# Block 2's feed-forwards: the second-matrix units moved apart, and other PSUM banks for them

## The reference, cut to what matters

```python
gate, up = jnp.split(x @ w_ffn_in[i], 2, axis=-1)      # 1024 -> 2 x 2816
ffn = (jax.nn.silu(gate) * up) @ w_ffn_out[i]          # 2816 -> 1024
x = layer_norm(ALPHA * x + ffn + ple, ln2_g[i], ln2_b[i])
```

## Time and profile before

| | us |
|---|---|
| median of three runs | 2522.41 |
| the profiled execution's own time | 2535.36 |
| its span, first to last instruction | 2533.6 |
| PE busy in the span | 2440.2 (96%) |
| DVE busy | 1771.5 (70%) |
| ACT busy | 1094.8 (43%) |
| POOL busy | 1067.2 (42%) |

### The profile page before, as it was taken

The page is one execution under the profiler, slowest core; times in us unless marked ns, Lnnn a source line. Parts: engine busy times, 40 slices in busy tenths (PEclk is TensorE's granted clock), DMA queues, the critical chain, the costliest instruction groups (busy, mean ns, idle before and its releaser), DMA issues.

```text
span 2533.6 us, 35157 instructions
## 1 busy us (share of the span) xinstructions
PE 2440.2 (96%) x13615; PEld 2044.6 (81%) x13615; DVE 1771.5 (70%) x2671; ACT 1094.8 (43%) x1803; POOL 1067.2 (42%) x600
## 2 busy tenths in 40 slices
PE   7999999999999999999999999999999999999997
PEld 5776788978776788998777779999877777999985
DVE  5677777864477687774587478887468747888856
ACT  4335532423425543443443554444444355444442
POOL 0332453424234244444245347544514534754441
PEclk9999999999999999999999999999999999999999
DMA  8613345543321433332232123332323111333321
GB/s 284 200 51 117 117 150 182 189 145 94 109 84 64 142 119 125 101 100 84 85 84 75 51 67 100 125 101 92 100 81 83 59 51 67 117 101 108 102 91 50
DMA packets 239645, 268.87 MB, mean 106 GB/s; under 512 B 19976, under 2 KB 204024, under 8 KB 239224
## 3 DMA queue, kind: packets, MB, share of 16 engines
q1 hardware_dynamic: 239480, 266.63, 32.6%
HBM read 264.51 MB, written 2.10 MB: 105 GB/s over the span
## 4 chain that ended last, share of the span: by engine, by line
PE 71%; DVE 12%; issue 5%; ACT 4%; POOL 4%; DMA 3%; SPq 0%; ACTq 0%; DVEq 0%; POOLq 0%
PE bank L2796 21%; PE bank L2798 21%; PE bank L2797 21%; DVE r L1905 2%; DVE m_cv L2246 2%; DVE k_lo L2054 1%; DMA raw<-in_ffn_w 1%; DMA raw<-in_w_ffn_in 1%; POOL w_lo L1650 1%; POOL k_lo L1661 1%; PE bank L3430 1%; DVE u_sum L2071 1%; ACT k_hi L1104 1%; DMA b_raw<-in_ada_w 1%; ACT w_hi L1050 1%
## 5 line engine op out<-in xcount | busy, mean ns | idle before, releaser
L1661 POOL TENSOR_TENSOR k_lo<-raw,k_hi 128x512 fp32r<-128x512 f32 x297 | 430.4, 1461 | 551.6 <-ACT k_hi L1104 550.5
L1650 POOL TENSOR_TENSOR w_lo<-raw,w_hi 128x2048 fp32r<-128x2048 f32 x53 | 248.7, 4692 | 536.6 <-ACT w_hi L1050 454.6
L1104 ACT ACTIVATE k_hi<-raw 128x512 fp32r<-128x512 f32 x444 | 270.9, 626 | 319.3 <-PE bank L2798 245.9
L2796 PE MATMUL bank<-h_hi,k_lo 128*128 128x256 f32 (+1 forms) x1156 | 371.4, 321 | 3.8 <-DVE k_lo L2054 2.5
L2797 PE MATMUL bank<-h_lo,k_hi 128*128 128x256 f32 (+1 forms) x1156 | 370.2, 320 | 0.0
L2798 PE MATMUL bank<-h_hi,k_hi 128*128 128x256 f32 (+1 forms) x1156 | 370.0, 320 | 0.0
L2796 PE MATMUL bank<-h_hi,w_lo 128*128 128x512 f32 x800 | 325.3, 407 | 8.8 <-DVE h_lo L2014 4.1
L2798 PE MATMUL bank<-h_hi,w_hi 128*128 128x512 f32 x800 | 314.1, 393 | 0.0
L2797 PE MATMUL bank<-h_lo,w_hi 128*128 128x512 f32 x800 | 314.1, 393 | 0.0
L2796 PE MATMUL bank<-f_hi,k_lo 128*128 128x512 f32 x704 | 278.1, 395 | 8.3 <-DVE u_row L2115 2.6
L2796 PE MATMUL bank<-u_t_hi,k_lo 128*128 128x256 f32 x1008 | 282.9, 281 | 1.5 <-POOL k_lo L1661 1.5
(11 more groups left out here) (401 smaller groups left out, 4956.8 us busy)
## 6 DMA issues: line engine op xcount, KB each, us to landing
raw<-in_ffn_w SPq DMA_DIRECT2D x56, 1024.0 KB, 5.4
raw<-in_w_ffn_in SPq DMA_DIRECT2D x44, 1024.0 KB, 5.1
raw<-in_w_in SPq DMA_DIRECT2D x34, 1024.0 KB
b_raw<-in_ada_w SPq DMA_DIRECT2D x32, 1024.0 KB, 5.4
f_raw<-in_w_ffn_out SPq DMA_DIRECT2D x24, 512.0 KB, 3.4
z_a<-in_ada_w SPq DMA_DIRECT2D x4, 2048.0 KB, 14.0
g_raw<-in_ada_w SPq DMA_DIRECT2D x8, 1024.0 KB, 5.2
raw<-in_w_out SPq DMA_DIRECT2D x8, 1024.0 KB
```

Of the source, the lines that this page charges most:

```text
L1104: act.activation(hi, src, ACT.Copy).then_inc(s.f_hi.up, 1)
L1650: pool.tensor_tensor(b.w_lo[p][:, 0:n], b.raw[p][:, 0:n], b.w_hi[p][:, 0:n].bitcast(F32), ALU.subtract)\
L1661: pool.tensor_tensor(lo, src, hi.bitcast(F32), ALU.subtract).then_inc(s.f_lo.up, 1)
L2796: pe.matmul(out, wlo, xhi, start=start, stop=False)
```

## The change

In block 2's plan (`spread` and not `early`) the first of a pair's two downs (j even) moves from behind the gate's unit to between the up side's unit and the gate's; the second (j odd) stays behind the gate's. The pairs concerned are 2 to 9. The order of a pair was "up side, gate, down, down" and becomes "up side, down, gate, down". Outside the tail a down with an even j now uses the banks 4 and 5, one with an odd j 3 and 7, and the plain units of the pairs 9 and 10 use 2 and 6. Plain 0, the Strassen units, the tail and the whole of block 1 keep order and banks. The buffers, the ring, `on_vector` and `summed` are unchanged code, but work on the new list.

```diff
         for i in range(PAIRS):
-            self.units += [("upper" if i in uppers else "plain", i, 0),
-                           ("whole" if early and i == 0 else "seven", i, 0)]
-            self.units += downs[:upto.get(i, 0)]
+            self.units.append(("upper" if i in uppers else "plain", i, 0))
+            inside = 1 if spread and not early and i in upto else 0
+            self.units += downs[:inside]
+            self.units.append(("whole" if early and i == 0 else "seven", i, 0))
+            self.units += downs[inside:upto.get(i, 0)]
             del downs[:upto.get(i, 0)]
...
-        if kind == "plain" and self.spread and not self.early and i == 0:
-            return 3, 7
+        if self.spread and not self.early and u < self.tail:
+            if kind == "plain":
+                return (2, 6) if i else (3, 7)
+            if kind == "down":
+                return (3, 7) if j % 2 else (4, 5)
         return first, first + 1
```

## The result

The changed kernel takes 2535.02 us, median of 7 runs (2530.01 to 2539.01); on the same chip the kernel before takes 2524.02 us, also of 7 (2521.05 to 2531.65). The ratio is 1.0037, with a 95% interval of 1.0020 to 1.0053: 5 to 13 us lost. That is within the 0.5% of "no change", but above the range of 2517 to 2531, and the 2524.1 forecast is 11 us too low.

What follows compares the result with a forecast made beforehand. The prediction took PE, busy 96% of the span, as the bound. Its terms, -1.95 + 0.5 + 3.2 = +1.7 us, put on the median of the runs, gave 2524.1 us, range 2517 to 2531, forecast as no change.

Steps and rivals of the forecast that it cites:

- seven 2's wait: PE's wait in seven 2 for a low part from POOL goes: 0.97 us per layer gained, 1.95 in all.
- transitions: Both downs of a pair now stand behind a Strassen unit: 0.03 us x 8 pairs x 2 layers, 0.5 us lost.
- plain 10's wait: Plain 10 waits for pair 9's products, delayed by seven 10's late load: 1.6 us per layer (0.3 to 2.6), 3.2 both.
- pairs 2 to 8: Steady order: PE's work unchanged, bank choice priced at nothing, DVE's slack hides the rest; nothing taken.
- clock behind a wait: Behind plain 10's wait: no clock term was forecast; nothing was taken beyond the wait itself.
- come just after the down's adds: In each half of a pair DVE's one set of sums follows the down's adds; 12.2 us of work before 15.4.
- Waits of PE for DVE's `x` adds (L2762) in every pair: Sign in the steady pairs that would prove the forecast wrong, as would any difference above 12 us.
- Nothing is given back: PE is full behind it: After plain 10's wait: the 3.2 us for both layers are not recovered, because PE is full.
- The rival in which the moved down waits in its middle: Pair 1's late low halves make the moved down wait about 1 us in both layers: +3.7, 2526.1 us; chance 0.17.
- 2 us were all there was to gain: From plain 0 to the tail PE is nearly full, so any order of units wins at most some 2 us.
- The prediction's estimate from the rule, 2.4 us a sum: By the shared-port lock a DVE sum could wait for a full POOL piece: 2.4 us each, 9.7 for four.
- a wait in every pair: Rival: DVE held by POOL in every unit, losing over 5.5 us per pair; +14, 2536 us at 6.5; chance 0.05.

Runs made afterwards that it cites:

- e7: The kernel before, order and banks untouched, with seven 2's four sums placed one piece earlier in DVE's order: 2528.14 us, ratio 0.9983.
- e3: The changed kernel with seven 8's sums one piece later, plain 10 on banks 3 and 7, the down before it on 0 and 4: 2523.14 us, ratio 0.9985.
- e1: The changed kernel with seven 8's four sums placed one piece later, behind the adds of the down before upper 8: 2533.84 us, ratio 1.0029.
- e6: The changed kernel's new order of downs with the banks of the kernel before: 2549.30 us, ratio 1.0076 to the kernel before.
- e5: e1 with 11 matmuls of the identity, into a bank nobody reads, in place of plain 10's wait: 2536.07 us, ratio 1.0020 to the kernel before.

## Why the prediction was wrong

By its own steps, per layer, with the total of both at the end:

| step | forecast | measured | both |
|---|---|---|---|
| seven 2's wait | -0.97 | -0.96, -0.99 | -1.95 |
| transitions | +0.25 | +0.13, +0.22 (the rest of the stretch) | +0.35 |
| plain 10's wait | +1.6 (0.3 to 2.6) | +2.47, +2.50 | +4.97 |
| pairs 2 to 8 | 0 | +1.62, +1.62 | +3.24 |
| clock behind a wait | 0 | +1.72, 0 | +1.72 |

**The step that failed** is "The pairs 2 to 8, in the steady order", and in it the sentence that in each half of a pair the sums "come just after the down's adds". I took the order of one pair for that of all. `summed` counts pieces, and where a pass has one pair the same count lands on the other side of the adds. Four sums of 0.68 us could have been borne there: M5 is due 4.27 us after the down's end (4.24 in the prediction), and the sums alone would have been done by 1740.86 + 2.7 = 1743.6. With POOL they took 6.9 us (1740.86 to 1747.73). The prediction had both numbers, the 1.77 us of a sum beside POOL and an upper's M5 on bank 3, and set them down as covered because it never walked the one pair where the piece count changes. It also named the sign, "Waits of PE for DVE's `x` adds (L2762) in every pair": it came in one pair only.

**Plain 10's wait** was found with the right mechanism, load and queue, and mis-sized: 2.5 for 1.6 us. The load landed at S + 6.5 (forecast 6.7); what was missing is one sum beside POOL, +1.1, which the bounds held and the value taken did not. (By the prediction's own prices two such sums would make 1.6 + 2.2 = 3.8 us; its bound of 2.6 is the case of one.) The reason given for the value, a chain "measured as a whole", was no reason: in the chain of before POOL was idle while the four sums ran (the first starts at 1794.78, the last is below), as POOL's next piece shows.

```profile
1796.71 0.68 DVE L2074 TENSOR_TENSOR u_sum<-raw,u_sum 128x512 f32<-128x512 f32 x1
...
1799.26 1.42 POOL L1661 TENSOR_TENSOR k_lo<-raw,k_hi 128x512 fp32r<-128x512 f32 x1 [6.84 <-ACT k_hi L1104]
```

**"Nothing is given back: PE is full behind it"** failed in the first layer, by 1.7 us: a unit that was full took longer, at the lower clock. The prediction had put that at nothing without a reason; a wait can cost more than itself.

The forecast is 10.9 us too low. Of these 6.6 are the terms above (+8.3 for +1.7), and 1.6 are the base: more runs moved the median of the kernel before from 2522.41 to 2524.02. The last 2.7 are within the interval of the ratio, and no run shows a place for them. The range, 2517 to 2531, was built on the runs' own spread around a forecast without these terms.

**What was right.** Seven 2's wait went in both layers. The prediction gave two reasons for it, the down in front and the new place of the sums; e7 shows that the second is enough alone. (One reading of the chain there was wrong: seven 2's M1 runs from 1576.41, so the two low parts at 1578.76 can't be "M1's and M7's"; M1's was done before. The 0.97 us don't depend on it.) The rival in which the moved down waits in its middle did not come: it takes 5.47 us in both layers. That 2 us were all there was to gain held: e3 and e7 leave PE without an idle moment and win 1.7 and 1.9. The transitions were small.

**The Trainium skill's rule**, "SBUF — State Buffer", section "SBUF: two separate sides", lets a VectorE operation with two SBUF inputs and a GpSimd one that reads SBUF hold the shared ports only in turn, each for a whole instruction. Above, sums beside POOL's low parts start 1.59 to 1.81 us apart, and POOL's pieces as far; a sum alone takes 0.68, and a low part 1.28 beside DVE's adds from PSUM (1747.76), together 1.96. So a sum and a low part at once take nearly as long as one after the other, and the trace comes near to the rule, with 0.2 to 0.3 us saved. The prediction's estimate from the rule, 2.4 us a sum, was too high against 1.7 to 1.8: it added to a sum's own 0.68 the 1.74 that a POOL piece takes beside DVE, where alone it takes 1.28. The rival that used it, a wait in every pair, did not come: DVE's busy time in the first layer's stretch grew by 13.4 us (242.93 against 229.50), some 1.7 us for each of the eight pairs 2 to 9, and the rival needed more than 5.5. A single place was enough.

## What to carry to other kernels

When an order of work is changed, walk the queue of every other engine through each irregular place (here the pass with one pair), not through the steady one; a rule that counts steps ahead changes its meaning where the steps change. Price a wait on a full engine with the other's queue at its contended durations, and add what the clock may cost behind it. And before units are moved to remove a wait, try whether moving the one late instruction does it: four sums one piece earlier gave all that this change could.

## What the runs showed of the hardware

A wait of TensorE can cost more than itself. The profiles of the changed kernel (two), of e1 and of e6 have eleven waits of 1.98 to 2.83 us in these stretches, counted as what the time from one unit's start to the next is too long. Behind six of them the granted clock was at 1.2 GHz for about 3.4 us, which cost 1.4 to 1.7 us more; behind five it stayed at 2.4 GHz. Behind the nine waits of 1.6 us (upper 8's in four profiles, one in e6) it never fell, nor anywhere in the stretches of e3, e5 and e7, where PE doesn't wait. Why the five went free stays open.
